# Other start addresses for four streamed buffers of a two-block kernel

## The reference

```
h = rmsnorm(x); proj = h @ w_in                  # 1024 -> 9232 columns
y_a = (bg * conv3(cg * xv)) @ w_a_out
y_b = gated_delta_rule(q, k, v, z, a, b) @ w_b_out
x = x + (sigmoid(ga) * y_a + sigmoid(gb) * y_b) @ w_o
up = conv3(rmsnorm(x) @ w_up)                    # 2 * 2816 columns
x = rmsnorm(x + (silu(gate) * val) @ w_down)
xn = rmsnorm(x); qa, ka, va, qr, kr, vr, gr, ta, tb = split(xn @ w_in_2)
x = x + (sigmoid(ta) * (attention @ w_proj_a_2) + sigmoid(tb) * (retention @ w_proj_b_2)) @ w_out_2
x = x + relu(rmsnorm(x) @ w_up_2) ** 2 @ w_down_2
```

## Time and profile before

| | us |
|---|---|
| median of 3 runs | 1178.58 (1178.16 to 1179.68) |
| the profiled execution, its own time | 1177.93 |
| its span, first to last instruction | 1176.1 |
| TensorE busy | 1134.2, 10250 matmuls |
| VectorE busy | 763.4 |
| ScalarE busy | 602.8 |
| GpSimd busy | 212.3 |

### The profile page before, as it was taken

How to read it: one execution, slowest core, us unless ns; L and a number is a source line. 1 busy time by engine, 2 the same in 40 slices (tenths; PEclk the granted TensorE clock), 3 DMA queues, 4 the chain that set the end, 5 groups by cost and what they waited for, 6 DMA issues and landing times.

```text
span 1176.1 us, 23223 instructions
## 1 busy us (share of the span) xinstructions
PE 1134.2 (96%) x10250; PEld 1102.9 (94%) x10250; DVE 763.4 (65%) x871; ACT 602.8 (51%) x688; POOL 212.3 (18%) x136
## 2 busy tenths in 40 slices
PE   5989999999999899999989999999999999999998
PEld 5878899999999899999979999999998999999998
DVE  5999785435455589788558857655565655665553
ACT  4879442342564466465556634433698444544341
POOL 3343263300131100000055600000011010311010
PEclk9999999999999999999999999999999999999999
DMA  6444333233354456555535554345543655555552
GB/s 239 168 144 143 121 140 109 74 108 121 131 196 163 162 195 203 196 199 194 179 139 180 180 182 174 113 142 179 179 142 110 215 191 174 198 192 200 194 187 101
DMA packets 27748, 192.81 MB, mean 164 GB/s; under 512 B 3072, under 2 KB 3200, under 8 KB 4992
## 3 DMA queue, kind: packets, MB, share of 16 engines
q1 hardware_dynamic: 27648, 191.33, 47.5%
HBM read 190.27 MB, written 1.05 MB: 163 GB/s over the span
## 4 chain that ended last, share of the span: by engine, by line
PE 72%; ACT 9%; DVE 9%; issue 5%; POOL 3%; DMA 2%; SPq 0%; POOLq 0%; ACTq 0%; DVEq 0%
PE psS L552 42%; PE psP L552 13%; PE psS L540 7%; ACT wh L883 4%; DVE wl L1204 3%; DVE acc L1210 2%; POOL t L1598 2%; DVE gdn L1204 1%; DMA raw<-in_wts 1%; PE psP L701 1%; PE psP L690 1%; DVE Xl L1210 1%; ACT L867 1%; PE psP L811 1%; PE psP L788 1%
## 5 line engine op out<-in xcount | busy, mean ns | idle before, releaser
L1204 DVE TENSOR_TENSOR wl<-raw,wh 128x2048 fp32r<-128x2048 f32 (+1 forms) x178 | 410.7, 2308 | 220.6 <-ACT wh L883 220.0
L883 ACT ACTIVATE wh<-raw 128x2048 fp32r<-128x2048 f32 x176 | 336.8, 1915 | 314.3 <-PE psS L552 160.6
L552 PE MATMUL psS<-Yh,wh 128*128 128x256 f32 x1056 | 301.7, 286 | 7.8 <-DVE Yl L1210 6.4
L552 PE MATMUL psS<-Yl,wh 128*128 128x256 f32 x1056 | 294.0, 278 | 0.0
L552 PE MATMUL psS<-Yh,wl 128*128 128x256 f32 x1056 | 293.9, 278 | 0.0
L552 PE MATMUL psS<-Xh,wh 128*128 128x256 f32 x896 | 261.7, 292 | 18.4 <-DVE wl L1204 13.5
L552 PE MATMUL psS<-Xl,wh 128*128 128x256 f32 x896 | 250.8, 280 | 0.0
L552 PE MATMUL psS<-Xh,wl 128*128 128x256 f32 x896 | 250.7, 280 | 0.0
L552 PEld LDWEIGHTS psS<-Yh,wh 128*128 128x128 f32 x1056 | 200.0, 189 | 11.7 <-DVE Yl L1210 7.2
L552 PEld LDWEIGHTS psS<-Yl,wh 128*128 128x128 f32 x1056 | 199.7, 189 | 2.6 <-issue 1.9
L552 PEld LDWEIGHTS psS<-Yh,wl 128*128 128x128 f32 x1056 | 199.2, 189 | 0.0
(11 more groups left out here) (238 smaller groups left out, 2004.9 us busy)
## 6 DMA issues: line engine op xcount, KB each, us to landing
raw<-in_wts SPq DMA_DIRECT2D x176, 1024.0 KB, 4.8
xT<-in_x SPq DMA_DIRECT2D x2, 512.0 KB, 6.1
raw<-in_wts SPq DMA_DIRECT2D x2, 512.0 KB, 7.2
gdn<-in_x SPq DMA_DIRECT2D x1, 1024.0 KB, 8.3
out<-xT SPq DMA_DIRECT2D x4, 256.0 KB, 2.1
xT<-in_sel SPq DMA_DIRECT2D x1, 512.0 KB, 6.5
xf<-in_dr SPq DMA_DIRECT2D x1, 512.0 KB, 7.0
xf<-in_md SPq DMA_DIRECT2D x1, 384.0 KB, 7.4
```

The costliest lines, as they stand in the source:

```text
L552: mm = pe.matmul(bank[:, half], a[:, n % 3, p, :], b[:, kk_, :], start=(first and i == 0), stop=(last and i == 2), skip_group_check=True)
L883: act.activation(wh[:, n % 3], raw[:, n % 2], ACT.Copy).then_inc(sem["wh"], 1)
L1204: return dve.tensor_tensor(out, a, b, op)
```

## The change

`Yh` and `Yl` become two parts of one wider tile `Y`, and `Xh` and `Xl` of a tile `X`, with some unused elements before, between and behind them. In bytes within 128 the starts are then: `Yh` 96, `Yl` 32, `Xh` 16, `Xl` 80. The tile `xf` is widened in the same way and begins where `Xh` begins. The tiles behind lie 384 bytes further on (24 and 72 elements of 4 bytes), which is three times 128, so their places within 128 bytes stay. `raw`, `wh`, `wl` and all others ahead don't move. Number, order and kind of the instructions are the same on every engine.

```diff
-        Yh, Yl = sb("Yh", [P, KT, S], F32R), sb("Yl", [P, KT, S], F32R)
+        def placed(t, *at):
+
+            return [t[:, a:a + KT * S].rearrange("p (k s) -> p k s", k=KT) for a in at]
+
+        Yh, Yl = placed(sb("Y", [P, 4120], F32R), 8, 2072)
 
 
         with ExitStack() as own:
-            Xh, Xl = sb("Xh", [P, KT, S], F32R, own), sb("Xl", [P, KT, S], F32R, own)
-        xf = sb("xf", [P, 4096])
+            Xh, Xl = placed(sb("X", [P, 4168], F32R, own), 28, 2092)
+        xf = sb("xf", [P, 4168])[:, 28:4124]
         dr = xf[:, 2048:3072].rearrange("p (h i) -> p h i", h=4)
         md = xf[:, 3072:3840].rearrange("p (g i) -> p g i", g=3)
         ST = [xf[:, a:a + 384] for a in (0, 384, 1024, 1408)]
```

## The result

The changed kernel takes **1204.47 us** (median of 4 runs, 1203.85 to 1205.03). The kernel before, run beside it on the same chip, takes 1178.99. The ratio is 1.0206, 95% interval 1.0185 to 1.0228: it is slower by 25.5 us, where 11.4 us less had been forecast.

A forecast was written before the change was run, and what follows sets the result against it. The prediction took TensorE's matmul pitch as the bound. With 11.4 us of slow pitch gone and all else costed at nothing, 1178.58 - 11.4 gave 1167.2 us, range 1150 to 1190 us.

The forecast's parts named there:

- What bounds the kernel: TensorE, busy 1134.2 of 1176.1 us; only the pitch of its matmuls could bring a large change, vector work costed at nothing.
- Two levels, 117.8 and 113.3 ns: Matmul pitches of the same code in the kernel before, 4.4 ns apart; start addresses could enter through the reading of streamed columns.
- the turns at 700.22 and 814.44: L540 slow turns into L552 fast, then L540 fast into L552 slow, as operands swap roles with nothing between.
- a lock needs each step to repeat the last; with a 64-byte hop in two of three steps it cannot persist: Likeliest case, 0.38: slow pitch between successive streams of Y and X ends, falling to the fast level, saving 11.4 us.
- The upper bound: Pitch slow everywhere with nothing saved: 5030 more slow matmuls, +22 us.
- All slow, 1201: Far end of the slower rival: every matmul at the slow pitch, 1201 us.
- another pitch altogether: Way to be wrong with the mechanism right: neither 113.3 nor 117.8 ns, stages of X and Y moving by different shares.
- Slower: the hop throws the stream into the slow level: Rival, 0.28: each 64-byte hop slows the matmul behind it, two of three of 7632, +11 us, 1189.5 us.
- means near 279 ns from 406 to 595 us: Sign of the hop theory: mean matmul durations near 279 ns in that stretch, where they were 276.
- No change: Rival, 0.26: start places have no effect, since 0 and 64 showed the same pitches; 1178.6 us.
- The fast level falls too: Rival, 0.08: different starts free half of the 6.6 ns loss on 6960 matmuls, 23 us beyond the 11.4, 1144 us.
- The size of the slow pitch in the kernel before: Summed over stages, 13.0 us of extra duration, taken as 2600 slow matmuls at 4.4 ns each, 11.4 us of pitch.

The follow-up runs named there:

- h1: Kernel before with wider tiles and a hole of 256 bytes between the halves of Y and of X, all tiles behind shifted by 512: 1179.89 us, ratio 1.0018.
- h3: Kernel before with an unused 128-byte tile between Yl and Xh, so Y stays at -64 and X, Z, O go to +64: 1190.26 us, ratio 1.0099.
- e1: Kernel before with Yh and Xh at 0, Yl and Xl at 64 bytes within 128, 64-byte hop kept: 1203.16 us, ratio 1.0183.
- g4: Kernel before with a 128-byte hole between the halves of Y and of X, places within 128 kept: 1197.11 us, ratio 1.0142.
- e2: Kernel before with both halves of Y and X at 96 bytes within 128, no hop: 1200.56 us, ratio 1.0168.
- e3: Kernel before with both halves of Y and X at 0 within 128, no hop: 1203.15 us, ratio 1.0185.
- h2: Kernel before with an unused 128-byte tile ahead of Yh, so all streams lie at distance +64: 1195.79 us, ratio 1.0134.
- g2: Kernel before with both halves of Y and X at 48 bytes within 128, no hop, weights at 0: 1200.83 us.
- g3: Kernel before with both halves of Y and X at 56 bytes within 128, no hop: 1205.67 us.
- f2: Kernel before with wh and wl at 64 and Y and X at 0 within 128 (Y +64, X -64, Z 0 modulo 256): 1193.35 us, ratio 1.0128.
- h4: Kernel before with an unused 64-byte tile ahead of wh, moving weights and streams together: 1180.08 us, ratio 1.0007.
- g1: Kernel before with only wl moved to 64 within 128, wh left at 0, all streams at one place: 1198.37 us, ratio 1.0152.
- e4: Kernel before with Y alone moved as in the change, X left in place in its tile: 1201.89 us, ratio 1.0174.
- f1: Kernel before with wh and wl moved to 64 within 128, streams left there, distance 0 everywhere: 1211.94 us, ratio 1.028.
- f4: Kernel before with both halves of Y and X at 72 bytes within 128, no hop: 1208.70 us.
- f3: Kernel before with both halves of Y and X at 32 bytes within 128, no hop, weights at 0: 1193.68 us.

## Why the prediction was wrong

**What bounds the kernel: right.** Only the pitch of TensorE could move the time, and only it did. Vector and scalar work on the moved tiles costs nothing: these busy times agree within 1 us, and TensorE has no new wait. `h1` with its wide tiles takes the time of before within 0.3%.

**Two levels, 117.8 and 113.3 ns, of which a start address decides something: right.** So was reading the turns at 700.22 and 814.44 in the earlier trace rows as a matter of addresses. Their reason is now plainer: with swapped roles the distance changes its sign, -64 becomes +64, and `h3` shows these two distances at two levels side by side.

**The step that failed: "a lock needs each step to repeat the last; with a 64-byte hop in two of three steps it cannot persist", and that streams would then fall to the fast level.** The pitches rose instead: the sum above 113.3 ns went from 12.1 to 45.4 us, where it was to go to nothing. A slow pitch came about with hops and without. In the streams of line 552, pieces at 113.3 ns are found in these kernels only for buffers at -64 or +64 whose halves have one place modulo 256. Take that from `X` and `Y` with a hop (`e1`, `g4`) or without one (`e2`, `e3`), and none of their blocks in the undisturbed stretch is fast. And a hop that keeps the distances (`h1`) leaves the levels as they were. I had taken 113.3 for the ground level because the stretch without side work ran at it. That stretch showed only what -64 does undisturbed. `h2` has the same code undisturbed at +64, and it stays at 117.8.

**The bound that was too near.** The upper bound let the slow pitch be 117.8 ns at most, because the rows of before have no other. The changed kernel has 118.8 for `X` and 119.9 for `Y` there, and `X` in `e1` has 120.8. "All slow, 1201" was therefore not the end; 1204.47 lies beyond. It also left out `Z` and `O` (below), and it took every ns of pitch to reach the total, while of 33.3 us only 26.8 did. That the result lies so near to 1201 is in part chance. The prediction did say that "another pitch altogether", different for `X` and `Y`, would make it wrong; that is what came. But no number had been put to it, and the range had been cut at 1190, with "all slow" left out as the far part of a rival.

**A detail that was wrong: "384 bytes, three times 128, so their places within 128 bytes stay".** They stay, but the period is 256, and three times 128 is 128 modulo 256. `Z` and `O` went from -64 to +64, and from 5.44 to 5.65 for 48. `Z` and `O` are 3 x (192 + 64 + 32) = 864 matmuls in groups by shape, so if all go from 113.3 to 117.7 ns, this is 3.8 us of pitch, which the starts in the trace confirm, in tiles of which the diff says nothing.

**The rivals.** "Slower: the hop throws the stream into the slow level" had the right side, and its sign, means near 279 ns from 406 to 595 us, was met and passed: 279, 281 and 285 in the groups shown above. But its mechanism isn't the main one: `e2` and `e3` without a hop are nearly as slow (1200.56 and 1203.15 us), and a hop of 256 costs at most 0.3%. What a hop adds to the distances of its two halves is seen only in single pitches (`X` in `e1`, `Y` in the change). "No change" argued that 0 and 64 had shown the same two levels. They had, and both were 64 away from the weights they met. The Trainium skill's page "SBUF — State Buffer", section "Who interferes with whom", on which that rival leaned (separate read ports for streams and weights, TensorE waiting on nobody), gives the distance between the two no part in the time. In this kernel it has one: with the same instructions, 1180.08 us at -64 and 1211.94 at 0. Whether the ports themselves meet or something behind them does, no run here can show. "The fast level falls too" didn't come: in no kernel do 24 matmuls in a row have a mean pitch below 113 ns.

**The size of the slow pitch in the kernel before, 2600 matmuls and 11.4 us: right; that it could be freed: not shown.** The starts in the trace of before give 12.1 us above 113.3 ns, and 2631 matmuls with a pitch over 115.5. The price of 4.4 ns a matmul is borne out too: `h3` has `X` and `Z` at 5.65 where they had 5.44, 0.21 us for 48. But no kernel lost this slow pitch.

**What stays open.** Why ±64 goes from one level to the other where side work (column sums, transposes) has come between, in both directions. Why `Z`, itself at -64, is fast behind `Y` at 119.9 in `e1` and slow in `g2`, `g3` and `g4`. Why `X` at -64 is slow between blocks of `Y` at +64 in `f2`, when `Y` at -64 is fast between blocks of `X` at +64 in `h3`. The level of a stream at ±64 depends also on what runs before it, in a way that these runs don't resolve. Why a mixture of two distances can be slower than both (`e1`). And what in the chip has a period of 256 bytes. Placing a buffer by block, so that it meets the faster sign after each piece of side work, wasn't tried; it may be a way to the 11.4 us.

## What to carry to other kernels

Where TensorE is the bound with full-rate float32 streams, read the pitch from the chain of work (us of a piece / its count) for every buffer, the untouched ones too, and write down modulo 256 bytes how far each streamed start lies from the stationary one: here -64 for all was best, and the other placements tried cost 1.0 to 2.8%. Any tile resized ahead of these buffers shifts all behind it, so in this kernel it pays to pad to multiples of 256. And where a trace shows two levels, don't take the faster one for the ground to which things fall when they are disturbed; give the case "slow everywhere, or slower still" a number and a place in the range.

## What was unexpected of the hardware

The pitch of a matmul of 256 float32 columns at full clock depends on the distance between its two operands in SBUF: in the stretch without side work around 500 us it is 113.3 or 117.8 ns at ±64 bytes modulo 256, 120.0 ns at 0, 118.8 at 128, 116.7 to 120.0 elsewhere. It depends on what runs before as well: 72 has 118.8 there and 121.0 later. Moving both operands by 64 bytes changed nothing (`h4`: 1.0007). A hole of 128 bytes between the halves costs 1.4%, all streams at +64 without a hole 1.3%, and a hole of 256 at most 0.3%. The levels come back to the hundredth: 336 matmuls of `Y` take 38.08 or 38.09 us in `h1`, `h3`, `h4`, 39.57 in `f2`, `g1`, `g4`, `h2`, and 40.30 to 40.33 in `e1`, `e3`, `e4`, `f1`, `f4`, `g3` and the changed kernel. Between them lie 39.20 (`f3`) and 39.76 (`e2`, `g2`). And a buffer's effect can be switched on by an unused tile of 128 bytes that no instruction ever reads or writes: 1.3% for a tile ahead of `Yh`, 1.0% for one behind `Yl`.
